# An attention layer turned round: queries, keys and gates with the rows of x on the partitions, two heads at a time

## The reference, cut to what matters

```python
def project(h):
    q, k, v, z = jnp.split(h @ w_in, [A_Q, A_Q + A_KVW, A_Q + 2 * A_KVW], axis=-1)
    q = _rmsnorm(q.reshape(B, T, A_HEADS, A_HD), qn)
    k = _rmsnorm(k.reshape(B, T, A_KV, A_HD), kn)
    ...
qx = _rope(qx, cos, sin)
kx = _rope(kx, cos, sin)
k_all = jnp.concatenate([kx, kc], axis=1)
v_all = jnp.concatenate([vx, vc], axis=1)
y_lat = (_attend(group(qx), k_all, v_all) * jax.nn.silu(zx)) @ w_out
```

## Time and profile before

| | us |
|---|---|
| median of 3 runs | 3566.31 |
| the profiled execution's own time | 3563.15 |
| its span in the trace | 3561.4 |
| TensorE busy | 3389.2 (95%) |
| values made, first key matmul | 1676.4 |
| first scores | 1764.56 |
| output projection starts | 2044.12 |
| its last block added to x | 2151.07 |

### The profile page before, as it was taken

One profiled execution on the slowest core, in us unless ns is written; L12 is line 12 of the kernel. 1 busy time (PEld: TensorE's weight loads), 2 busy tenths in 40 slices (PEclk: granted clock), 3 DMA queues, 4 the chain that ended last, 5 costly groups with the idle time before them and its releaser, 6 DMA issues.

```text
span 3561.4 us, 47179 instructions
## 1 busy us (share of the span) xinstructions
PE 3389.2 (95%) x18976; PEld 2869.1 (81%) x18976; DVE 2242.8 (63%) x3404; ACT 1323.1 (37%) x1969; POOL 1595.0 (45%) x800
## 2 busy tenths in 40 slices
PE   8899998999999999998899889999999999999999
PEld 3577686788888888787788788998899889789889
DVE  6899798778978875655688734448344554432333
ACT  3322224322222232324355534444434444443443
POOL 1144476544444544566465532444345234444443
PEclk9999998999999999999999999999999999999999
DMA  8676575445544544684566664556544346555555
GB/s 305 222 231 222 171 235 173 127 145 171 159 145 148 176 154 130 205 285 139 173 230 226 201 185 141 171 184 184 177 145 141 113 147 191 177 183 185 189 183 172
DMA packets 193274, 644.68 MB, mean 181 GB/s; under 512 B 22064, under 2 KB 34448, under 8 KB 193056
## 3 DMA queue, kind: packets, MB, share of 16 engines
q1 hardware_dynamic: 139680, 455.68, 39.3%
q10 hardware_dynamic: 51264, 180.38, 15.9%
q0 software_dynamic: 2112, 5.61, 0.5%
HBM read 624.81 MB, written 14.68 MB: 180 GB/s over the span
## 4 chain that ended last, share of the span: by engine, by line
PE 75%; DVE 13%; ACT 4%; POOL 3%; issue 3%; DMA 3%; ACTq 0%; DVEq 0%; POOLq 0%
PE PS L346 14%; PE PS L348 14%; PE PS L347 14%; PE PS L389 3%; PE PS L391 3%; PE PS L390 3%; DVE WR L1502 3%; PE PS L837 3%; PE PS L838 3%; PE PS L839 3%; POOL WL L2324 3%; DMA WR<-ada_w 2%; DVE JUNK L1502 2%; PE PS L585 2%; ACT WH L935 2%
## 5 line engine op out<-in xcount | busy, mean ns | idle before, releaser
L2324 POOL TENSOR_TENSOR WL<-WR,WH 128x1024 fp32r<-128x1024 f32 x530 | 1381.4, 2607 | 1720.4 <-ACT WH L935 1719.8
L346 PE MATMUL PS<-HTH,WH 128*128 128x256 f32 (+1 forms) x4192 | 1363.0, 325 | 62.7 <-POOL WL L2324 30.0
L347 PE MATMUL PS<-HTL,WH 128*128 128x256 f32 (+1 forms) x4192 | 1332.8, 318 | 0.0
L348 PE MATMUL PS<-HTH,WL 128*128 128x256 f32 (+1 forms) x4192 | 1332.4, 318 | 0.0
L935 ACT ACTIVATE WH<-WR 128x1024 fp32r<-128x1024 f32 x753 | 793.8, 1058 | 1371.5 <-PE PS L348 720.5
L346 PEld LDWEIGHTS PS<-HTH,WH 128*128 128x128 f32 x4192 | 806.0, 192 | 153.9 <-POOL WL L2324 38.4
L347 PEld LDWEIGHTS PS<-HTL,WH 128*128 128x128 f32 x4192 | 806.7, 192 | 57.0 <-issue 6.7
L348 PEld LDWEIGHTS PS<-HTH,WL 128*128 128x128 f32 x4192 | 805.9, 192 | 51.2
L1480 DVE TENSOR_TENSOR WL<-WR,WH 128x1024 fp32r<-128x1024 f32 x223 | 293.4, 1316 | 435.1 <-ACT WH L935 434.8
L1502 DVE CUSTOM_DVE_ANT_0 WR<-WR,SCB 128x1024 f32<-128x1024 f32 x160 | 312.1, 1951 | 58.1 <-DMA WR<-ada_w 54.1
L1502 DVE CUSTOM_DVE_ANT_0 WR<-WR,SCB,MOD 128x1024 f32<-128x1024 f32 x160 | 318.2, 1989 | 44.2 <-DMA WR<-ada_w 34.9
(11 more groups left out here) (322 smaller groups left out, 3474.1 us busy)
## 6 DMA issues: line engine op xcount, KB each, us to landing
WR<-ada_w SPq DMA_DIRECT2D x320, 512.0 KB, 4.8
WR<-e_gu SPq DMA_DIRECT2D x128, 512.0 KB, 4.1
WR<-m_vo ACTq DMA_DIRECT2D x64, 512.0 KB, 3.9
WR<-n_m SPq DMA_DIRECT2D x64, 512.0 KB, 4.0
WR<-e_d SPq DMA_DIRECT2D x64, 512.0 KB, 4.8
AR<-ada_p SPq DMA_DIRECT2D x48, 512.0 KB, 6.0
WR<-f_gate ACTq DMA_DIRECT2D x32, 512.0 KB, 4.5
WR<-f_out ACTq DMA_DIRECT2D x32, 512.0 KB, 4.6
```

Source lines behind the costliest of these rows:

```text
L346: e.matmul(ps[:, 0:n], wh[:, k, :], xh, start=c == 0, stop=False)
L347: e.matmul(ps[:, 0:n], wh[:, k, :], xl, start=False, stop=False)
L348: i = e.matmul(ps[:, 0:n], wl[:, k, :], xh, start=False, stop=c == K - 1)
L2324: e.tensor_tensor(WL[:, s % NP, :], WR[:, plan["slot"][plan["split"][s]], :], WH[:, s % NP, :].bitcast(F32), ALU.subtract).then_inc(*L.up( ...
```

## The change

Keys are made by `tproject` with rows on the partitions; so are queries and gates, two heads at a time (256 + 256 columns, one job `("qz", j)` of 8 pieces). The sum of squares is ScalarE's (`accum_out`). The rotation is VectorE's, by reading pairs in reversed order from PSUM with tables that hold the gains. The root goes into the exponential's scale instead of the queries; the softmax's division and the gate go into one operation on the result. TensorE then transposes keys, queries and each head's result. The small steps of the pair before are run between the pieces of the next pair (`between`), the last pair's between the pieces of output blocks 0 to 3, which become one job `("out4",)` of 8 pieces by `kproject`. The result goes to columns 0:256 of `HH_`/`HL_`; x stays in `YT` and is not reloaded.

```diff
         def values(h):
-                for s_ in range(4):
-                    i = e.matmul(ps[:, 0:256], A_VT[:, s_, 128 * g:128 * g + 128], A_PT[h % 2][:, s_, :],
-                                 start=s_ == 0, stop=s_ == 3)
+                for tb in range(2):
+                    t = slice(128 * tb, 128 * tb + 128)
+                    for s_ in range(4):
+                        i = e.matmul(ps[:, t], A_PT[h % 2][:, s_, t], A_VT[:, s_, g], start=s_ == 0, stop=s_ == 3)
...
+            def steps(j):
...
+                return {0: at0, 1: lambda: turn_queries(j), 2: lambda: scores(a), 3: lambda: scores(b),
+                        4: lambda: turn_rows(a), 5: at5, 6: lambda: values(a), 7: at7}
...
+            tproject(("av",), I["a_v"], 2, ALL)
+            tproject(("ak",), I["a_k"], 2, ALL, wrk)
+            tproject(("qz", 0), I["a_qz"][0], 2, LAT, between={5: keys(0), 6: keys(2)})
+            for j in range(1, 8):
+                tproject(("qz", j), I["a_qz"][j], 2, LAT, between=steps(j - 1))
+            kproject(2, [("out", 2, n) for n in range(4)], I["a_out4"], CTX, "ys", last_steps())
```

`at0` transposes the result of the pair's second head (`turn_head(a - 1)`), `at7` is `values(b)` and `turn_head(a)`. ScalarE:

```diff
+            w.wait_ge(L.at(("full", ("ak",))))
+            for tb in (2, 3, 0, 1):
+                for g in range(4):
...
+                    e.activation(A_JUNK[n % 8], place[("ak", tb)][:, 128 * g:128 * g + 128], ACT.Square, scale=1.0,
+                                 accum_out=A_KS[:, n:n + 1]).then_inc(*L.up(act_done, ("ksq", tb)))
+            w.wait_ge(L.last(act_done))
+            e.activation(A_KS, A_KS, ACT.Sqrt, bias=EPSC[:], scale=1.0 / 128).then_inc(*L.up(act_done, "ks"))
...
+            def pair(j):
+                w.wait_ge(L.at(("full", ("qz", j))))
...
+                for tb in range(2):
+                    for i in range(2):
+                        e.activation(A_JUNK[n], ps[:, 128 * i:128 * i + 128], ACT.Square, scale=1.0,
+                                     accum_out=A_QS[j % 2][:, n:n + 1]).then_inc(
...
+                    e.activation(A_Z[j % 2][tb], ps[:, 256:512], ACT.Tanh, scale=0.5).then_inc(
...
+                e.activation(A_QS[j % 2], A_QS[j % 2], ACT.Sqrt, bias=EPSQ[:], scale=1.0).then_inc(
...
+                for q in range(8):
+                    cut_to(s0 + q + NP)
+                    if q == 0 and j > 1:
+                        head(a - 1)
+                    elif q == 1:
+                        turned_queries(j - 1)
+                    elif q == 2:
+                        exponentials(a)
...
+                    elif q == 7:
+                        head(a)
+                pair(j)
```

VectorE (its `rope` is two products from PSUM and an addition `tt(dst, dst, tmp, ALU.add)`; `pair(j)` is two of them, the two gates, which free the banks, and a small reciprocal):

```diff
-            for g in range(4):
-                along(("ak", g))
-                if g:
-                    rope(("ak", g - 1), 512, A_KT[:, g - 1, :], [])
-                bg(4)
...
-            for h in range(14):
...
-                bg(2)
...
-                bg(2)
+            bg(4)
...
+            bg(4)
...
+            for q in range(7):
...
+                bg(1)
+            pair(0)
+            for j in range(1, 8):
...
+                for q in range(8):
...
+                    if q < 7:
+                        bg(1)
+                bg(1 if j < 7 else 0)
+                pair(j)
```

More of the change, by code:

```diff
@@ L356, in hproject, with kproject @@
             project(job, halves(src), b - a, lambda c: (HH_[:, c, a:b], HL_[:, c, a:b]), ("h", tag))
-        def kproject(tag, jobs, sources, cols):
+        def kproject(tag, jobs, sources, cols, ready="h", between=()):
             a, b = cols
+            between = dict(between)
             banks = [acc(job) for job in jobs]
-            for q, s in enumerate(weights(("first", tag), [sources[n] for n in range(8)])):
+            for q, s in enumerate(weights(("out4",) if tag == 2 else ("first", tag), [sources[n] for n in range(8)])):
                 wh = WH[:, s % NP, :].rearrange("p (k n) -> p k n", n=512)
@@ L600, in attn @@
         def attn():
[L601 to L611, removed]
@@ L647, in values, with turn_head @@
                 i.then_inc(*L.up(mm_done, ("full", ("ao", h)), ("pt_used", h)))
[L649 to L662, removed]
+            def turn_head(h):
+                ps = wrk(("yt", h))
+                for tb in range(2):
+                    w.wait_ge(L.at(("yr", h, tb)))
+                    i = e.transpose(ps[:, 128 * tb:128 * tb + 128], A_Y[h % 2][:, 128 * tb:128 * tb + 128], IDN[:])
+                i.then_inc(*L.up(mm_done, ("full", ("yt", h)), ("y_used", h)))
@@ L1241, in attn, with head @@
[L1241 to L1245 removed]
+            def head(h):
+                w.wait_ge(L.at(("full", ("yt", h))))
+                e.activation(HH_[:, h, 0:256], place[("yt", h)][:, 0:256], ACT.Copy, scale=0.5).then_inc(
+                    *L.up(act_done, ("yh", 2, h)))
+            s0 = plan[("qz", 0)][0]
+            for q in range(7):
+                cut_to(s0 + q + 1 + NP)
+                if q in (2, 3):
+                    scaled_keys([2, 3] if q == 2 else [0, 1])
+                elif q in (5, 6):
+                    turned_keys(2 * q - 9)
@@ new lines, in attn @@
+            w.wait_ge(L.at(("full", ("ak",))))
+            for tb in (2, 3):
+                w.wait_ge(L.at(("ksq", tb)))
+                rope(A_KN[tb], place[("ak", tb)][:], 4, A_CK[:, tb - 2:tb - 1, :], A_SK[:, tb - 2:tb - 1, :], A_TK, ("kroped", tb),
+                     ("free", ("ak", tb)))
+            for tb in (0, 1):
+                w.wait_ge(L.at(("ksq", tb)))
+                tt(A_KN[tb].rearrange("p (h n) -> p h n", h=4), place[("ak", tb)].rearrange("p (h n) -> p h n", h=4),
+                   over(A_GAIN[2], 4), ALU.mult, ("kroped", tb), ("free", ("ak", tb)))
@@ new lines, in attn, with turned_keys, pair @@
+            w.wait_ge(L.at("ks"))
+            recip(A_KS, A_KS, "kscale")
+            def turned_keys(g):
+                w.wait_ge(L.at(("full", ("kt", g))))
+                copy(A_KT[:, g, :], place[("kt", g)][:], ("kte", g), ("free", ("kt", g)))
+            def pair(j):
+                w.wait_ge(L.at(("full", ("qz", j))))
+                for tb in range(2):
+                    w.wait_ge(L.at(("tanh", "z", j, tb)))
+                    rope(A_QR[j % 2][tb], place[("qz", j, 2 + tb)][:, 0:256], 2, A_CQ[:, tb:tb + 1, :], A_SQ[:, tb:tb + 1, :],
+                         A_TQ[tb], ("qr", j, tb))
+                for tb in range(2):
+                    z = A_Z[j % 2][tb]
+                    stt(z, z, 1.0, place[("qz", j, 2 + tb)][:, 256:512], ALU.add, ALU.mult, ("free", ("qz", j, 2 + tb)))
+                w.wait_ge(L.at(("qroot", j)))
+                recip(A_QS[j % 2], A_QS[j % 2], ("qs", j))
@@ new lines, in attn @@
+            s0 = plan[("out4",)][0]
+            for q in range(8):
+                cut_to(s0 + q + NP)
+                if q == 0:
+                    head(12)
+                    head(13)
+                elif q == 1:
+                    maxima(14)
+                elif q == 2:
+                    maxima(15)
+                elif q == 3:
+                    turned(14)
+                elif q == 4:
+                    turned(15)
+                    values(14)
+                elif q == 5:
+                    values(15)
+                    head(14)
+                elif q == 6:
+                    head(15)
@@ L2360, in outproject @@
         def outproject(tag, sq):
-            for n in range(NB):
+            for n in range(4 if tag == 2 else 0, NB):
                 along(("out", tag, n))
```

394 lines of the change are left out of this document (231 added, 163 removed).

## The result

The changed kernel takes 3556.79 us as the median of ten runs (3550.06 to 3559.42), the kernel before 3566.08 beside it (3560.3 to 3570.01): a ratio of 0.9973, 95% interval 0.9963 to 0.9982. That is 9.3 us less, where 25 were forecast. The profiled execution has a span of 3554.7 (3561.4 before).

A forecast was written before the change was run, and what follows sets the result against it. It took the head loop as bound by conversion. Stages of 81.0, 240.8 and 122.5 made 444.3 us against 474.7, 30.4 less; 6.6 lost in layer 3 left -23.8, forecast 3541, range 3527 to 3555.

The forecast's parts named there:

- What bounds the kernel before: Head loop: bound by conversion through ScalarE and GpSimd, 17.3 us a head, against 16.6 of TensorE work.
- a lock against shared bandwidth: VectorE and GpSimd: port pair locked per instruction, so passes within ScalarE's 1.55 us cost nothing; shared bandwidth would always cost.
- Stage 1: Keys and first pair: 81.0 us against 88.2 before, with a TensorE pause of 7 to 9 us after the keys.
- Stage 2: Seven pairs of heads: 34.4 us a pair, 240.8 in all, against 35.0 for two heads before.
- I charge nothing on the ring: Seven pairs: background passes on VectorE add no time, mostly finding GpSimd's WL begun and running in ScalarE's 1.55 us.
- The ring: Each pair: TensorE 25.4, ScalarE's head-end 4.5, copy and WL 3.95, hand-overs 0.6, together 34.4 us.
- Rival (a): Seven pairs: the head-end hides and a pair falls to 31.6 us, 20 more gained, 3521; chance 0.14.
- Rival (c): Seven pairs: all single passes start just before GpSimd, 39.7 us a pair, 37 more, 3578; chance 0.08.
- Rival (b): Seven pairs: TensorE goes cold in every pair, losing some 3.5 us each, 24 in all, 3565; chance 0.12.
- Rival (d): Values matmuls: 128 columns cost as much as 256, 28 us more in all, about 3568; chance 0.04.
- Stage 3: After the seven pairs, to the last block added to x: 122.5 us against 107.0, with some 5 us idle starting `out4`.
- Layer 3: Start of layer 3: four background halves left instead of two, taking 9.4 us and moving the reciprocal by 6.6 us.

The follow-up runs named there:

- e14: The kernel before, with the 52 background passes of heads 0 to 12 narrowed to 64 of 1024 columns: 3550.97 us, ratio 0.9962.
- e2_scalar: The changed kernel with the product of maximum and root's reciprocal made by tensor_scalar with a per-partition scalar operand: 3540.92 us, ratio 0.9929.
- e3_four: The changed kernel with one background half more in each of output blocks 4 to 7, none left for layer 3: 3550.35 us, ratio 0.9956.
- e13_both: e2_scalar with the background passes of the pairs also narrowed to 64 columns: 3535.81 us, ratio 0.9918.
- e12_all: e11_sum with the WL of each pair's third piece on VectorE, between rotations and gates: 3508.92 us, ratio 0.9844.
- e10_adds: e2_scalar with output blocks 0 to 3 added before VectorE makes the WL of that stretch's eleventh piece: 3534.88 us, ratio 0.9916.
- e9_outdve: e2_scalar and e3_four together, with all WLs of output blocks 4 to 15 on VectorE: 3521.9 us, ratio 0.9879.
- e11_sum: e9_outdve and e10_adds together, without the pass ahead of each pair, and ten background halves in blocks 4 to 13: 3528.01 us, ratio 0.9893.

## Why the prediction was right and wrong

**What bounds the kernel before: right.** In the kernel before TensorE waits 0.5 to 1.0 us for a WL in nearly every head. e14 shows the rest: with passes out of the way a head is 16.9, all of it TensorE's, where I had added up 16.6. My test of a lock against shared bandwidth was none, since a pass that falls between two WLs costs nothing either way; what speaks for the lock is that whoever comes first keeps its own time.

**Stage 1: right** (80.1 against 81.0), by errors that cancel. The pause on TensorE is 4.65, not 7 to 9: key squares of 128 with their sums took 5.4 us instead of 7.2, and the root needed no load of a table. Later waits of 0.7 to 1.0 at four places ate that.

**Stage 2: the step that failed is "I charge nothing on the ring".** The sentence ahead of it, that passes "mostly find the WL begun and then run in ScalarE's 1.55", was a guess on order of arrival. In the changed kernel 53 WLs average 2.75, and the pairs take 13.2 us more than forecast; 36.3 is off 34 by more than the 2 us that I had named as the sign of being wrong. The guess would have come out with one other line: in e2_scalar the passes do find WL begun, all but one in eight, and the pair is 33.5. So the second half of the failure is an operation that I left out of the sum: the product L1568, 128 x 1. I listed VectorE's rotations and additions and took the small ones at nothing. The row showed the wait after the fact (2.29 us). The Trainium skill (SBUF — State Buffer, section "SBUF: two separate sides") names among VectorE's operations that take the shared pair those with two SBUF inputs; I had cited it for the passes and didn't hold the added operations against it one by one. The traces agree: 0.71 us in the mean with two streamed operands, 0.21 with one and a per-partition scalar.

The same rule was waiting at the queries' addition, which the prediction called covered: 2.12 instead of 0.42 us in e2_scalar, and 1.64 of it on TensorE.

The order in the changed kernel isn't firm either. e3_four has the same code in its pairs, and its execution takes 252.0 us from the first root to the last, with pairs of 34.6 to 37.5, where this one takes 255.2.

The ring (ScalarE's head-end, the copy, its WL, TensorE's pieces and steps up to the next head-end) was overrated by 1.4 us a pair: with passes and product gone (e13_both) it gives 33.0, not 34.4. ScalarE's head-end takes 3.6 instead of 4.5, and 16 matmuls of 128 columns for the values 1.70 instead of 1.88. Rival (a), 31.6 from a hidden head-end, exists: e12_all's 31.9, but only after that head-end's WL was moved to the other engine.

**Rival (c), passes ahead of GpSimd, was the right mechanism at half its price.** I gave it 0.08 and 39.7 us a pair for every WL hit. In the pair shown 5 of 8 WLs were hit, and with a mean of 2.75 the WLs cost 3.0 us a pair more than unhindered ones, not 6.4. **Rival (b), cold pairs,** came in three of seven pairs (half clock for about 3 us at 1924, 1962 and 2000), 0.9 us each: 37.2 against 36.3. The idle time ahead was 1.97 to 2.03 us there; after 2.01 us (1887.56) and after 3.57 us (1762.38) the granted clock stayed at 1.00, so the two rows of the prediction gave no measure. **Rival (d)** is out: the values cost 1.70.

**Stage 3: 2.6 us over.** The start was as told (4.68 idle). The unforeseen term is the wait of 4.29 for a bank, with its matmuls at half clock; e10_adds removed it and won 4.7 us. When four accumulators end at one time, what empties them is on the path.

**Layer 3: right,** 6.66 against 6.6: from the first pass to the reciprocal 9.5 us, 9.4 forecast, with the wait of 4.00 for the third load in it. e3_four gave 7.1 us back.

**Behind and ahead of the layer.** The last block is added 18.75 us earlier, layer 3 starts 12.1 earlier, yet the end comes only 6.7 earlier. From the first matmul of layer 3 to the end the changed kernel takes 1407.0, the kernel before 1401.6, with the same work: 9294 matmuls in both, in which TensorE is busy 3.2 us longer in the changed kernel. Part of it is seen in the later attention block, at a head of its queries: 48 matmuls of 256 columns in 7.4 us in the changed kernel, 5.9 in the kernel before. Stretches of the one, then the other:

```profile
2460.10:2463.60 3.50, 3.50 (x17) 3.50 (x18) 3.07 (x5) 0.33 (x2) 0.00 (x0) 0.53 0.64 199
```
```profile
2469.90:2475.80 5.90, 5.86 (x49) 5.86 (x50) 4.07 (x6) 2.64 (x4) 0.00 (x0) 1.00 0.51 178
```

The granted clock is 0.53 for 3.5 us, after 2.87 idle; in the kernel before 1.37 of idle stood there and the clock stayed. It isn't caused by the change: e14_before_narrow, the kernel before in all but the narrow passes, takes 1407.6, while e2_scalar takes 1401.7, and all the others 1405 to 1408. Likewise ahead of the layer: this execution was 3.3 us early at 1628, and the root of the keys, with the same work before it, lies between 1722.0 and 1729.4 in the twelve traces that have it. A stage's place in the span is good to some 5 us. Its length is firm where the order of arrival is (e2_scalar, e9_outdve and e10_adds have 237.5 us from the first root to the last), and not in the changed kernel (252.0 and 255.2). Which of these differences recurs in every execution stays open.

**The sum.** Forecast 30.4 less for the layer, found 15.5: 0.9 better in stage 1, 13.2 and 2.6 worse in stages 2 and 3. With 6.7 for layer 3, 3.3 for the early start and 5.4 behind, the span is 6.7 less. The last step of my sum also had a slip: 3539.4 and 3.2 make 3542.6, not 3541.

## What to carry to other kernels

When VectorE and GpSimd work side by side, go through every VectorE operation with two streamed SBUF operands, the smallest too, and ask who arrives first; a per-partition scalar in place of a one-column operand took 16 us off this kernel. Blocked background work is cheap and background work that comes first is dear: look at which of the two rows is longer than it is alone, not at VectorE's busy share. Less work can cost time: the pass dropped in e11_sum, forecast at 0 to 1.6 us won in a pair, cost 1.8 there. So a sum of parts has to be run.

## What the runs showed of the hardware

A VectorE operation on one element per partition waited out a GpSimd operation of 2.39 us, for 2.29, and the 64-column passes of e14_before_narrow took 1.39 in the mean for one form. An activation with a sum costs about 0.45 us for 256 columns and in pairs here a 128-column one every 0.25. A stretch at half clock followed an idle time of TensorE of 1.97 us in the changed kernel, and none followed one of 3.57 there or one of 2.89 in the kernel before; one costs 0.9 to 1.5 us. The same work behind the layer took 1401.6 to 1407.6 us in single executions of these kernels; that spread is nearly as large as the 6.7 us between the two profiled spans. How much of it comes from such stretches isn't shown.
